# Scatter matmuls of the expert loop split by token tile, and stage borders handed over bank by bank

## The reference

```
# first block
h = x + 0.5 * rms_norm(swiglu(rms_norm(x)))            # stage A, d_ff 2816
h = h + rms_norm(hybrid_mixer(rms_norm(h)) @ w_out)     # stage B, forgetting attention + gated delta rule
h = h + rms_norm(memory_cross_attention(...) @ w_o)     # stage C
h = h + 0.5 * rms_norm(swiglu(rms_norm(h)))             # stage D
# second block, modulated: mod = silu(c) @ w_ada + b_ada, in six parts
h = h + g1 * (merged(conv, diff_attention) @ w_out)     # stage E
h = h + g2 * (routed(h2) + shared(h2))                  # stage F, 64 experts, top 8, expert width 256
```

## Time and profile before

| | us |
|---|---|
| median of 3 runs | 1688.07 |
| lowest, highest | 1686.02, 1689.14 |
| the profiled execution | 1686.85 |
| its span | 1685.1 |
| PE busy, share of the span | 1578.4, 94% |
| DVE, ACT, POOL busy | 712.1, 451.9, 44.1 |

### The profile page before, as it was taken

One profiled execution on the slowest core, in us unless ns is written; L12 is line 12 of the kernel. 1 busy time (PEld: TensorE's weight loads), 2 busy tenths in 40 slices (PEclk: granted clock), 3 DMA queues, 4 the chain that ended last, 5 costly groups with the idle time before them and its releaser, 6 DMA issues.

```text
span 1685.1 us, 26269 instructions
## 1 busy us (share of the span) xinstructions
PE 1578.4 (94%) x10058; PEld 1056.1 (63%) x10058; DVE 712.1 (42%) x1232; ACT 451.9 (27%) x729; POOL 44.1 (3%) x96
## 2 busy tenths in 40 slices
PE   6999989999998899998999989978998999999997
PEld 6999878668666499996854444554444444444443
DVE  4555346355213355554499754461121221212212
ACT  4333333141101243334001261022221222222221
POOL 5000000100000000000100000000000000000000
PEclk9999979999999999998999999979999999999999
DMA  9755473311331736446444462319997896988984
GB/s 317 268 174 175 150 252 113 125 51 51 128 135 65 251 128 206 161 163 238 167 150 150 150 225 75 134 54 358 340 389 293 326 362 211 338 326 294 343 324 167
DMA packets 154788, 350.78 MB, mean 208 GB/s; under 512 B 11615, under 2 KB 56879, under 8 KB 154160
## 3 DMA queue, kind: packets, MB, share of 16 engines
q1 hardware_dynamic: 151440, 342.98, 56.7%
q0 software_dynamic: 1792, 3.09, 0.7%
q10 hardware_dynamic: 1440, 3.17, 0.5%
HBM read 579.83 MB, written 2.16 MB: 345 GB/s over the span
## 4 chain that ended last, share of the span: by engine, by line
PE 44%; DVE 9%; DMA 6%; ACT 3%; SPq 3%; issue 2%; DVEq 0%; ACTq 0%
PE bank L2688 9%; PE bank L664 8%; PE bank L1963 6%; PE bank L2714 6%; DVE arena L2169 6%; PE bank L644 4%; PE bank L2621 3%; DMA ring<-in_w_exp_down 3%; DMA ring<-in_w_exp_gu 2%; PE bank L1954 2%; PE bank L484 2%; SPq L2937 2%; PE bank L2600 2%; ACT xn L2905 1%; PE bank L2580 1%
## 5 line engine op out<-in xcount | busy, mean ns | idle before, releaser
L664 PE MATMUL bank<-x_high,w_high 128*128 128x256 f32 x704 | 200.9, 285 | 6.1 <-DVEq L251 6.1
L664 PE MATMUL bank<-x_low,w_high 128*128 128x256 f32 x704 | 200.5, 285 | 0.0
L664 PE MATMUL bank<-x_high,w_low 128*128 128x256 f32 x704 | 199.5, 283 | 0.0
L1963 PE MATMUL bank<-ring,xT 128*128 128x512 f32 x384 | 168.3, 598 | 11.2 <-ACT arena L2326 11.2
L736 DVE TENSOR_TENSOR w_low<-ring,w_high 128x2048 fp32r<-128x2048 f32 x60 | 137.4, 2292 | 77.2 <-ACT w_high L701 77.2
L664 PEld LDWEIGHTS bank<-x_high,w_high 128*128 128x128 f32 x704 | 133.9, 190 | 7.6 <-issue 6.9
L1963 PEld LDWEIGHTS bank<-ring,xT 128*128 128x128 f32 x384 | 73.2, 192 | 102.5 <-issue 102.5
L664 PEld LDWEIGHTS bank<-x_high,w_low 128*128 128x128 f32 x704 | 135.2, 192 | 0.0
L664 PEld LDWEIGHTS bank<-x_low,w_high 128*128 128x128 f32 x704 | 134.2, 191 | 0.7
L2714 PE MATMUL bank<-ring,arena 128*32 128x512 f32 x1024 | 119.4, 607 | 14.9 <-DMA ring<-in_w_exp_down 7.1
L701 ACT ACTIVATE w_high<-ring 128x2048 fp32r<-128x2048 f32 x60 | 114.5, 1912 | 61.8 <-PE bank L644 59.2
(11 more groups left out here) (523 smaller groups left out, 2297.5 us busy)
## 6 DMA issues: line engine op xcount, KB each, us to landing
ring<-in_w_exp_gu SPq DMA_DIRECT2D x512, 512.0 KB
ring<-in_w_exp_down SPq DMA_DIRECT2D x128, 1024.0 KB
ring<-in_w_in SPq DMA_DIRECT2D x42, 768.0 KB, 5.8
ring<-in_ffn_w_gate SPq DMA_DIRECT2D x22, 1024.0 KB, 5.6
ring<-in_ffn_w_up SPq DMA_DIRECT2D x22, 1024.0 KB, 8.7
ring<-in_ffn_w_down SPq DMA_DIRECT2D x21, 1024.0 KB, 10.1
ring<-in_w_ada SPq DMA_DIRECT2D x24, 768.0 KB, 5.8
ring<-in_w_in SPq DMA_DIRECT2D x21, 512.0 KB, 6.8
```

What stands on the lines that cost most here:

```text
L664: ins = pe.eng.matmul(bank[:, k * S:(k + 1) * S], ff_w[f][w][:, c, k, :], (x_high, x_low)[x][:, c, :], start=c == 0 and i == 0, stop=c == ...
L1963: ins = mm(ps[b][:], lhs[:, c, t * P:(t + 1) * P], w[:, c, :], start=c == 0, stop=c == DC - 1 and bias is None)
```

## The change

Five edits, all in order and semaphores; the arithmetic is the same but for the order in which the residual multiplies.

1. `scatter(i, t)` takes one tile. Tile 0 stays behind the gate and up products; tile 1 and behind it `owners(i + 1)` go behind the second `pick`, ahead of the down products.
2. The last `second` of `pe_ff` orders its 24 matmuls by tile, and `down_done` is raised once for each tile, so ACT may square tile 0 while PE makes tile 1.
3. `act_bank_norm` puts after each square too. `vec_residual` multiplies each bank by the gain as soon as it was squared, into a place in `arena`; after the root it takes the reciprocal and makes `h = scaled * reciprocal + h` in one instruction of 1024 columns.
4. `pe_mods` no longer waits at its end; each pair of transposes of tile 0 in `pe_tiles_to_features` waits for the one bank that it writes.
5. In stage B's DVE list, two small memsets go behind `vec_norm`.

```diff
-    def vec_residual(v, bank):
+    def vec_residual(v, bank, start, order):
         g = v.gain()
-        for t in range(T):
-            tiles = [bank(t, n) for n in range(2)]
+        scaled = view(arena, start, (T, D))
+        for t, n in order:
+            at = slice(n * 512, (n + 1) * 512)
             v.answer()
-            v.do(v.eng.reciprocal(stat[:, 16 + t:17 + t], stat[:, 14 + t:15 + t]))
-            for n in range(2):
-                at = slice(n * 512, (n + 1) * 512)
-                v.do(v.eng.scalar_tensor_tensor(xn[:, t, at], tiles[n][:],
-                                                stat[:, 16 + t:17 + t], g[:, at],
-                                                ALU.mult, ALU.mult))
-            v.do(v.eng.tensor_tensor(h[:, t], h[:, t], xn[:, t], ALU.add))
-            v.ask()
+            v.do(v.eng.tensor_tensor(scaled[:, t, at], bank(t, n)[:], g[:, at], ALU.mult))
+            if n:
+                v.answer()
+                v.do(v.eng.reciprocal(stat[:, 16 + t:17 + t], stat[:, 14 + t:15 + t]))
+                v.do(v.eng.scalar_tensor_tensor(h[:, t], scaled[:, t], stat[:, 16 + t:17 + t],
+                                                h[:, t], ALU.mult, ALU.add))
+                v.ask()
...
     # act_bank_norm, behind each Square
+            a.put()
...
     # pe_tiles_to_features, ahead of each transpose
+                if pe.mods_before is not None and t == c % 2 == 0:
+                    assert banks[c // 2] == MOD_BANKS[c // 2]
+                    pe.eng.wait_ge(mod_free, pe.mods_before + c // 2 + 1)
...
     # second(), in pe_ff
+            order = [(f, t) for f in range(2) for t in range(T)]
+            for f, t in sorted(order, key=lambda x: x[1]) if last else order:
...
-            ins.then_inc(down_done, 1)
+                if f == 1 and (last or t == T - 1):
+                    ins.then_inc(down_done, 1)
...
     # dense(), act_part
-            a.eng.wait_ge(down_done, NF)
-            act_bank_norm(a, ff_bank, 0.5, BY_TILE)
+            def bank(t, n):
+                a.eng.wait_ge(down_done, NF + t)
+                return ff_bank(t, n)
+
+            act_bank_norm(a, bank, 0.5, BY_TILE)
...
     # pe_mods
-        pe.eng.wait_ge(mod_free, pe.mods.n)
+        pe.mods_before = pe.mods.n - len(MOD_BANKS)
...
     # stage F, pe_part
                 if i:
-                    scatter(i - 1)
-                if i + 1 < STEPS:
-                    owners(i + 1)
+                    scatter(i - 1, 0)
                 if more:
                     wait(picks_set, q + 2)
                     pick(q + 1, 2 * half)
...
                 if more:
                     pick(q + 1, 2 * half + 1)
+                if i:
+                    scatter(i - 1, 1)
+                if i + 1 < STEPS:
+                    owners(i + 1)
                 wait(down_in, 16 * LANES * (i + 1))
```

More of the change, by code:

```diff
@@ L220, in __init__ @@
             self.block = self.sets = 0
+            self.mods_before = None
         def slot(self):
@@ L461, in pe_tiles_to_features @@
                     ins.then_inc(psum_full, 1)
+        pe.mods_before = None
     def pe_to_features(pe, src, chunks):
@@ L507, in pe_product, with vec_product_residual @@
             pe_tokens(pe, lhs)
[L509 to L518, removed]
+    def vec_product_residual(v, start):
+        vec_residual(v, lambda t, n: ps[v.hand()], start, BY_HALF)
         v.give_back(4)
@@ L639, in second @@
             pe.eng.wait_ge(low_set[2], b + 1)
[L640 to L648, removed]
-            ins.then_inc(down_done, 1)
+            order = [(f, t) for f in range(2) for t in range(T)]
+            for f, t in sorted(order, key=lambda x: x[1]) if last else order:
+                for i, (w, x) in enumerate(PAIRS):
+                    for m in range(2):
+                        ins = pe.eng.matmul(
+                            ff_bank(t, m)[:], ff_h[x][:, a % 2, f, t * P:(t + 1) * P],
+                            (last_down if last else ff_w[2])[w][:, f, m * 512:(m + 1) * 512],
+                            start=first and f == 0 and i == 0,
+                            stop=last and f == 1 and i == 2, skip_group_check=True)
+                if f == 1 and (last or t == T - 1):
+                    ins.then_inc(down_done, 1)
         for a, j in rounds(pe.eng, n, PEEL):
@@ L787, in vec_part @@
             vec_ff(v, tag, NF, base[0])
-            vec_residual(v, ff_bank)
+            vec_residual(v, ff_bank, ff_end + 2 * PIECE, BY_TILE)
         def act_part(a):
@@ L1321, in vec_part @@
             tt, ts, cp = e.tensor_tensor, e.tensor_scalar, e.tensor_copy
+            vec_norm(v, h)
             do(e.memset(qkvP[:, :, 0:PAD], 0.0))
             do(e.memset(bias16[:, 8:12], 0.0))
-            vec_norm(v, h)
             vec_to_features_shared(v, xT, DC, preg[:, 1])
@@ L1516, in vec_part @@
                 e.sem_inc(gdn_features, 1)
-            vec_product_residual(v)
+            vec_product_residual(v, 0)
         def act_part(a):
@@ L1806, in vec_part @@
             cut_ahead["vec"](v)
-            vec_product_residual(v)
+            vec_product_residual(v, 12288)
         def act_part(a):
@@ L2612, in owners, with scatter @@
                 ins.then_inc(own_full, 1)
-            def scatter(i):
+            def scatter(i, t):
                 wait(y_low_set, 2 * (i + 1))
                 wait(seated_set, i + 1)
[L2618 to L2623, removed]
+                for n in range(2):
+                    for part in (y_high, y_low):
+                        mm(ps[2 * t + n][:], seated[i % 2][:, t * P:(t + 1) * P], part[:, n, :],
+                           start=False, stop=False, skip_group_check=True)
             few = slice(0, N_EXP)
```

## The result

| | before | after |
|---|---|---|
| median of 4 runs, us | 1688.59 | 1658.03 |
| lowest, highest | 1686.02, 1689.14 | 1653.47, 1658.54 |
| the profiled execution | 1686.85 | 1653.47 |
| its span | 1685.1 | 1651.8 |
| mean granted TensorE clock | 0.971 | 0.978 |

The ratio is 0.9823, 95% interval 0.9804 to 0.9841: faster by 30.6 us. The forecast was 21, and its range ended 1 us above what came.

What follows compares the result with a forecast made beforehand. PE bounds the kernel, alternating with loads in stage F and pausing at borders. Loop 8.8, A to B 6.0, D to E 5.4, C to D 1.05, less 0.7 for the clock: 20.5 us, so 1667 us, range 1659 to 1676.

Steps and rivals of the forecast that it cites:

- the loop term: Stage F loop: 17 steps keeping 0.50 us each, plus 0.3 for the last two steps, 8.8 us, bounds 3 and 13.
- the clock terms: Clock gains of 1.5 us at A to B and 1.0 at D to E, less 0.7 for another fall in the loop.
- 17 x 0.50: Stage F loop: 17 of 31 steps keep a saving of 0.50 us between scatter's start and the down products, 8.5 us.
- the upper bound that the prediction gave: Stage F loop: the saving in one step is at most 0.60 us, with 0.24 as lower bound.
- each late load cost its step, some two: Stage F loop: 8 or so late loads and newly late ones take away the saving of 12 to 18 steps.
- the bound of 25: Stage F loop: at most 25 steps keep the saving, from scatter's share of the chain; the lower bound was 13.
- 1.5: A to B border: gain from the clock for transposes and narrow matmuls, 1.5 us, between -1.5 and 5.
- 1.0: D to E border: gain from the clock, 1.0 us, between 0 and 2.5.
- the clock stays up: Rival, both borders: clock gains 5 and 2.5 us instead of 1.5 and 1.0, loop at 10, 1661 us; chance 0.13.
- The loads take the loop's gain: Rival, stage F loop: loads leave 3.5 us of gain instead of 8.8, 1672.5 us; chance 0.12.
- The transposes overtake DVE: Rival, loop: hidden-value transposes outrun their 0.83 us cover, each 0.1 beyond costing 3.1 us, so slower; chance 0.04.
- No load came to set the opening of B or E: Stages B and E: a load setting the start would take up to all that border's gain; no-change rival, chance 0.04.

Runs made afterwards that it cites:

- loop only: The kernel before with edit 1 alone (scatter in two parts, owners behind the second): 1672.26 us, ratio 0.9925 to the kernel before.
- The pair without reloads: The kernel before and the changed kernel, each with no lane loaded again after step 0: 1665.6 us (ratio 0.9881) and 1629.06 us (0.9675).
- owners late: The kernel before with only owners moved behind the second pick, scatter left whole and early: 1676.49 us, ratio 0.9943 to the kernel before.
- no reloads before: The kernel before with no lane loaded again after step 0: 1665.6 us, ratio 0.9881 to the kernel before.
- whole down: The changed kernel with edit 2 undone (last down products by half, one release at their end): ratio 0.9903 to the kernel before.
- one wait: The changed kernel with edit 4 undone (PE waits for all four modulation banks ahead of the transposes): ratio 0.9841 to the kernel before.
- scatter all late: The changed kernel with both parts of scatter and owners behind the second pick: 1659.94 us, ratio 0.9858 to the kernel before.
- the halves: The kernel before with edit 1 alone (1672.26 us, ratio 0.9925), and the changed kernel with the old loop (1667.5 us, ratio 0.9892).

## Why the prediction missed

The direction held, and so did what edit 1 and the borders were to do. Two sizes did not: the loop term, 8.8 where the medians show 14.0, and the clock terms, 2.5 less 0.7 where the profiles show about 7.

**Loop, the term "17 x 0.50".** Both factors were too small. PE's order saves 0.60 in a step, the upper bound that the prediction gave. Its steps were right (half a scatter 1.03 for 1.02, the first pick 0.94 for 0.96, transposes and second pick 1.18 for 1.16, the other half 1.02 for 1.01) but for owners: they take 0.24 to the next start when a pick on the full array follows, and 0.15 when the equally narrow down products do. I had carried the 0.24 over and so allowed too little for two changes of shape fewer. The split was off as well: 0.40 for the stop and 0.10 for the shapes, where it is 0.30 and about as much. The number of steps is the less certain factor. By the medians 23 steps' worth is kept, near the bound of 25; the interval of loop only reaches from 15 to 27 steps, and its lower end is the term that I had. I had let each late load cost its step, some two. The pair without reloads has 4.9 us taken in all. A reading that fits is that a late load is released by PE's own work: its release comes earlier as well, and only what PE saved behind the release turns into a wait. No run isolates it. 14 instead of 8.8 explains 5 us of the 10.

**Clock, the terms "1.5" and "1.0".** The positions came as worked out: transposes 4.67 us earlier at A to B (forecast 4.5), squares of tile 1 at 207.86 in place of 210.21, the pause at C to D 1.2 us shorter (forecast 1.05). But A to B gained 3.3 us more by the first wide matmul of B, and B a further 1.6, where the fall at 334 us did not come; D to E gained 2.0 beyond its 4.5. That is 7 us that go with the clock in these two executions, where I had 2.5 less 0.7.

How much of it holds beyond them? At D to E the clock fell in all five profiles without edit 2 (before, loop only, owners late, no reloads before, whole down) and in none of the eight with it, edit 4 alone undone and edit 3 alone undone among them. At A to B it is at the lower level for 17.1 us in three of the five and for 13.7 in two (in loop only in two pieces); with edit 2 for 6.8 us in five and 10.2 in three. That gain is there each time. Inside B there is no such rule: it falls in four of the five and in two of the eight. The 18.7 us of medians for the borders, with an interval from 14.0 to 22.4, are near the profile's 17.

It comes nearest to the rival "the clock stays up", to which I gave 0.13; with the loop at 10 it had 1661. But that rival held whole only at D to E, since at A to B the clock still fell, and part of B's share is luck. Where I went wrong is in taking a value for the clock between the ends instead of asking what PE's pauses do to it: at D to E whole down (pauses of 1.86 and 0.64 us around its first transposes) loses it, and one wait (one pause of 1.41) does not. That is one profile of each, so it is a sign and not a threshold.

**Rivals.** The loads take the loop's gain: 5 of 19 us by the medians; by the profiles 7 in the mean, and 3 to 14 between single ones. The transposes overtake DVE: the cover is there, and scatter all late shows what it prevents. No load came to set the opening of B or E; PE's wait there is still for DVE.

Together: 20.5 plus 5 (loop) plus 5 (clock) is 30.5, against 30.6 in the medians. The agreement is partly luck, since the one 5 is from medians and the other from one pair of profiles; the medians of the halves add up to 32.7. That the time fell outside the range, by 1 us, took both sizes: either one alone would have left it inside.

## What to carry to other kernels

Sum a border twice: once for the pause that goes, once for the work at the half clock behind it. Here the second was about 7 us beside 10 of the first. At D to E the fall of the clock was gone in every profile and at A to B it was shorter in every one; further behind, it was chance. In a loop that sometimes waits for loads, time both orders with the loads taken away before discounting a saving: here some three quarters of it were kept by the medians. And a wait that a row prints can be shorter than what it costs, or stand below what the view prints; the starts of neighbouring groups tell. Filling one pause with work on constants moved the fall of the clock and shortened it, and gave no time that could be measured.

## What was not expected of the hardware

- With only sixteen transposes and waits for 4.6 us at D to E, the granted clock stayed at 1.00, in eight profiles of eight, and the wide matmuls behind them ran at the full level.
- Behind a pause it came back from 0.50 to 1.00 after sixteen transposes and ahead of any other matmul (loop only at 222.2 us). At C to D the same holds in three profiles; in the changed kernel's it took D's wide matmuls (0.50 from 576.7 to 586.9).
- The granted clock can differ between executions of one order: in B it fell at 336.6 for 6.8 us in one profile and not in another, and behind the same pause of 4.50 us at A to B the narrow matmuls took 7.01 us once and 4.15 another time.
- Two changes fewer between 32-column tiles and the full array, ahead of the first pick's end, saved about 0.19 us in a step.
